# A decoder layer with a product-key expert layer: U and V rows of three token blocks gathered as pairs into 18 slots, their weighted sums on TensorE

## What is computed

```
q = (xt @ w_query).reshape(T, 8, 2, 128)
s = einsum('thcd,hckd->thck', q, sub_keys)
top_s, top_i = top_k(s, 16)                    # per head and half of the query: the 16 best of 128 keys
cand_s = top_s[:, :, 0, :, None] + top_s[:, :, 1, None, :]
best_s, pos = top_k(cand_s, 16)                # 16 of 256 pairs: 16 experts out of 16384, per head
gate = softmax(best_s)
u = expert_u[expert_idx]; h = gelu(einsum('cd,ced->ce', xc, u))
out = einsum('ce,ced->cd', gate * h, expert_v[expert_idx])
x = layer_norm(alpha * x + out)
```

## Time and profile before

| | |
|---|---|
| median of three runs | 1891.44 us |
| span of the profiled execution | 1889.7 us |
| PE, DVE, POOL, ACT busy | 67%, 68%, 57%, 13% |
| DMA engines, packets of the gathers | 77.2% of 16 engines' span |
| all DMA | 603.28 MB, mean 319 GB/s |
| granted PE clock, mean | 0.82 |

### The profile page before, as it was taken

How to read it: one execution, slowest core, us unless ns; L and a number is a source line. 1 busy time by engine, 2 the same in 40 slices (tenths; PEclk the granted TensorE clock), 3 DMA queues, 4 the chain that set the end, 5 groups by cost and what they waited for, 6 DMA issues and landing times.

```text
span 1889.7 us, 14555 instructions
## 1 busy us (share of the span) xinstructions
PE 1258.4 (67%) x3056; PEld 582.3 (31%) x3056; DVE 1289.4 (68%) x2842; ACT 238.6 (13%) x570; POOL 1073.2 (57%) x1253
## 2 busy tenths in 40 slices
PE   6778979563789776456666565665656565566665
PEld 3565446231346432122222221222222222222221
DVE  1348988789668866666767676767576667666556
ACT  0110000112111111011100111100101011111110
POOL 0004344335446667657767666667676767667774
PEclk9889989676989888777777878777877887778787
DMA  7668787857589889889999998899999999899996
GB/s 267 239 245 321 300 316 278 295 181 277 212 284 386 296 311 365 313 313 355 360 348 356 345 363 308 322 352 349 361 349 344 348 369 335 323 345 358 350 369 262
DMA packets 180946, 603.28 MB, mean 319 GB/s; under 512 B 18720, under 2 KB 21024, under 8 KB 180768
## 3 DMA queue, kind: packets, MB, share of 16 engines
q0 software_dynamic: 147456, 536.94, 77.2%
q1 hardware_dynamic: 33440, 65.80, 9.6%
HBM read 600.57 MB, written 2.10 MB: 319 GB/s over the span
## 4 chain that ended last, share of the span: by engine, by line
PE 24%; issue 20%; DVE 18%; DMA 17%; POOL 15%; another core or an unknown queue 1%; ACT 1%; POOLq 1%; DVEq 0%; SPq 0%; ACTq 0%
POOL ring L376 14%; DMA ring<-peer_v,stage 10%; PE ACC L428 9%; DVE ring L953 6%; PE W L483 6%; DMA ring<-peer_u,stage 6%; PE W L489 2%; PE W L659 2%; PE X L631 2%; DMA wt<-w_in 1%; PE ACC L631 1%; PE W L631 1%; DVE best_i L1207 1%; DVE xs L1001 1%
## 5 line engine op out<-in xcount | busy, mean ns | idle before, releaser
L428 PE MATMUL ACC<-ring,diag 128*128 128x512 f32 x1272 | 783.5, 774 | 476.6 <-DMA ring<-peer_v,stage 442.1
L953 DVE SCALAR_TENSOR_TENSOR ring<-ring,X 128x1024 f32<-128x1024 f32 x512 | 613.3, 1219 | 316.0 <-DMA ring<-peer_u,stage 288.1
L376 POOL DMA_INDIRECT ring<-peer_u,stage x512 | 522.1, 1020 | 410.1 <-DVE ring L953 214.1
L376 POOL DMA_INDIRECT ring<-peer_v,stage x512 | 503.0, 982 | 246.0 <-issue 153.8
L428 PEld LDWEIGHTS ACC<-ring,diag 128*128 128x128 f32 x1272 | 298.5, 248 | 956.7 <-issue 889.8
L771 ACT ACTIVATE diag<-ident,gate 128x128 f32<-128x128 f32 x318 | 122.8, 399 | 895.3 <-PE ACC L428 627.2
L1001 DVE SCALAR_TENSOR_TENSOR xs<-ring,gate,xs 128x1024 f32<-128x1024 f32 x96 | 123.3, 1284 | 53.6 <-DMA ring<-peer_v,stage 45.0
L483 PE MATMUL W<-wt,actT 128*128 128x512 f32 x320 | 143.9, 607 | 12.6 <-DMA ident<-ident_in 11.5
L659 PE MATMUL W<-actT,wt 128*128 128x128 f32 (+1 forms) x512 | 116.4, 389 | 1.4 <-ACT actT L833 1.4
L973 DVE SCALAR_TENSOR_TENSOR xs<-ring,gate,xs 128x512 f32<-128x512 f32 x98 | 73.3, 748 | 47.8 <-DMA ring<-peer_v,stage 45.7
L659 PEld LDWEIGHTS W<-actT,wt 128*128 128x128 f32 x512 | 80.1, 198 | 36.7 <-issue 2.7
(11 more groups left out here) (180 smaller groups left out, 804.3 us busy)
## 6 DMA issues: line engine op xcount, KB each, us to landing
wt<-w_in SPq DMA_DIRECT2D x14, 2048.0 KB
wt<-peer_w_query SPq DMA_DIRECT2D x8, 2048.0 KB
wt<-w_out SPq DMA_DIRECT2D x4, 2048.0 KB
ring<-peer_u,stage POOLq DMA_INDIRECT x512
ring<-peer_v,stage POOLq DMA_INDIRECT x512
out<-xs SPq DMA_DIRECT2D x4, 512.0 KB, 5.4
actT<-xT SPq DMA_DIRECT2D x1, 1536.0 KB, 11.7
xs<-x SPq DMA_DIRECT2D x1, 1536.0 KB, 14.1
```

What stands on the lines that cost most here:

```text
L376: pool.indirect_dma_start(out=ring[:, r, :], out_offset=None, in_=table, in_offset=bass.IndirectOffsetOnAxis(ap=stage[:, half, c:c + 1], a ...
L428: last = nc.tensor.matmul(ACC[:, half * HW:(half + 1) * HW], diag[:, odd, m, :], ring[:, r, half * HW:(half + 1) * HW], start=start and m ...
L953: STT(out=ring[:, r, :], in0=ring[:, r, :], scalar=1.0, in1=X[:], op0=ALU.mult, op1=ALU.mult, accum_out=hid[:, bass.ds(e, 1)]).then_inc(sl ...
```

## The change

**Tables.** U and V are laid side by side in one table `uv` of 16384 x 2048 floats before the launch. The kernel sees it as 32768 rows of 4 KB, with U of expert e in row 2e and V in row 2e + 1; the index is doubled by one more small DVE instruction per quarter, and a V gather has `element_offset` 1024.

**Buffers.** One `arena` of 18 slots of 8 KB per partition. The mixer's buffers and the ring of 8 are views of it. Once the mixer and block 0 are done with them, the slots are used for blocks 1 to 3.

**Block 0** keeps the ring, now for all its 16 groups of V rows; the last five have three rows on PE and five on DVE.

**Blocks 1 to 3** are 384 pairs. For each, POOL issues a U gather into the first half of a slot and a V gather into the second, both with the index read straight from `idx`, with one wait per pair (`pairs_summed` of the pair 18 before). DVE takes the dot. After four pairs (`FG`) ACT takes the GELU of four columns, DVE multiplies them by the gates (`weigh`, placed behind the first dot of the next group), ACT makes four diagonals in a ring of six (`ND`), and PE adds all four V rows. DVE adds no V row of these blocks. The steps that find experts lie between groups of four.

```diff
+V_GROUPS = E // RING
+AT_V = U_GROUPS
+ALONE = 11
+
+
+
+NF = (NB - 1) * E
+NS = 18
+EARLY, LATE = 6, 14
+FG = 4
+ND = 6
...
         wt = sb("wt", [P, NW, KD, HW])
...
-        ring = sb("ring", [P, RING, D])
-        attn = sb("attn", [P, 3 * HW])
+        arena = sb("arena", [P, NS * 2 * D])
+        fused = [arena[:, i * 2 * D:(i + 1) * 2 * D] for i in range(NS)]
...
+        keys = part(7 * K, K, "p (c n) -> p c n", c=HC)
+        wt = part(8 * K, 4 * K, "p (i k n) -> p i k n", i=NW, k=KD)
+        actT = part(12 * K, 2 * K, "p (k t) -> p k t", k=KD)
+        ring = part(14 * K, 4 * K, "p (r d) -> p r d", r=RING)
...
         ACC = ctx.enter_context(nc.psum_tensor("ACC", [P, D], fp32))
+        X2 = W[:, 0:2, :].rearrange("p a n -> p (a n)")
+        ACC2 = W[:, 2:4, :].rearrange("p a n -> p (a n)")
+
+        def token_of(b):
+
+            return X2 if b == 2 else X[:]
+
+        def sum_of(b):
+
+            return ACC2 if b % 2 else ACC[:]
...
+                    pool.indirect_dma_start(
-                    one_table(peer_u, quarter * QUARTER + j * RING, n, j % 2, n)
+                    one_table(0, quarter * QUARTER + j * RING, n, j % 2)
             for i in range(V_GROUPS):
                 n = AT_V + i
-                one_table(peer_v, i * RING, n, n % 2, n)
-            with pool.Fori(0, MIXED // PERIOD) as quarter:
-                pool.wait_ge(experts_ready, quarter + 5)
-                for j in range(PERIOD):
-                    both_tables(quarter * QUARTER + (E + j * HALF), quarter * QUARTER + (E - LAG + j * HALF),
-                                quarter * PERIOD + (AT_MIXED + j), (AT_MIXED + j) % 2,
-                                quarter * (2 * PERIOD) + (AT_MIXED + 2 * j))
-            for i in range(TAIL):
-                n = AT_TAIL + i
-                one_table(peer_v, NB * E - LAG + i * RING, n, n % 2, AT_MIXED + 2 * MIXED + i)
+                one_table(D, i * RING, n, n % 2)
+            for n in range(NF):
+                slot = n % NS
+                if n % QUARTER == 0:
+                    pool.wait_ge(experts_ready, 4 + n // QUARTER + 1)
+                if n == 0:
+                    pool.wait_ge(mixer_ready, 2 * NB)
+                elif n == EARLY:
+                    pool.wait_ge(keys_scored, 4 + 3 * WQ)
+                elif LATE <= n < NS:
+                    for r in (2 * (n - LATE), 2 * (n - LATE) + 1):
+                        pool.wait_ge(slot_used[r], AT_V + V_GROUPS + 1)
+                elif n >= NS:
+                    pool.wait_ge(pairs_summed, n - NS + 1)
+                pool.indirect_dma_start(
+                    out=fused[slot][:, 0:D], out_offset=None, in_=rows,
+                    in_offset=bass.IndirectOffsetOnAxis(ap=idx[:, E + n:E + n + 1], axis=0),
+                ).then_inc(pair_landed[slot], 16)
+                pool.indirect_dma_start(
+                    out=fused[slot][:, D:2 * D], out_offset=None, in_=rows,
+                    in_offset=bass.IndirectOffsetOnAxis(ap=idx[:, E + n:E + n + 1], axis=0),
+                    element_offset=D,
+                ).then_inc(second_landed[slot], 16)
...
+            def add_pairs(b):
+
+                if b > 1:
+                    pe.wait_ge(sum_read, b - 1)
+                for n in range((b - 1) * E, b * E):
+                    first, last_one = n % E == 0, n % E == E - 1
+                    pe.wait_ge(pair_diag_ready, n + 1)
+                    pe.wait_ge(second_landed[n % NS], 16 * (n // NS + 1))
+                    for half in range(2):
+                        last = nc.tensor.matmul(
+                            sum_of(b)[:, half * HW:(half + 1) * HW], fdiag[:, n % ND, :],
+                            fused[n % NS][:, D + half * HW:D + (half + 1) * HW], start=first, stop=last_one)
+                    last.then_inc(pairs_summed, 1)
...
+            beside(range(2 * ALONE + sum(BESIDE_QUERY), 2 * V_GROUPS))
+            for b in range(1, NB):
+                add_pairs(b)
 
...
-                if b:
-
-                    last_dot(b * 4 - 1)
                 if b == 1:
                     act.wait_ge(x1_taken, 2 * NB)
+                elif b == 2:
+                    act.wait_ge(scores_stored, 4 + 3 * WQ)
+                elif b == 3:
+                    act.wait_ge(pair_dotted, E)
                 for half in range(2):
-                    last = nc.scalar.activation(X[:, half * HW:(half + 1) * HW], xs[:, b, half * HW:(half + 1) * HW],
...
+            def gate_exp(q):
+
+                cols = slice(q * QUARTER, (q + 1) * QUARTER)
+                act.wait_ge(experts_ready, q + 1)
+                nc.scalar.activation(gate[:, cols], gate[:, cols], ACT.Exp).then_inc(pair_gate_ready, 1)
+
+            def pair_group(g):
+
+                cols = slice(E + g * FG, E + (g + 1) * FG)
+                act.wait_ge(pair_dotted, (g + 1) * FG)
+                nc.scalar.activation(hid[:, cols], hid[:, cols], ACT.Gelu).then_inc(pair_gelu_ready, 1)
+                act.wait_ge(pair_weighed, g + 1)
+                for n in range(g * FG, (g + 1) * FG):
+                    if n == 0:
+                        act.wait_ge(slot_used[PE_SLOTS[-1]], AT_V + V_GROUPS + 1)
+                    elif n >= ND:
+                        act.wait_ge(pairs_summed, n - ND + 1)
+                    nc.scalar.activation(fdiag[:, n % ND, :], ident[:], ACT.Copy,
+                                         scale=gate[:, E + n:E + n + 1]).then_inc(pair_diag_ready, 1)
 
             project(0, WAVES[0])
...
-                mixed_diagonals(first, first + 1)
-                gelu(q - 1, q)
-                mixed_diagonals(first + 1, first + 2)
-                act.wait_ge(weights_ready, q - 3)
-                mixed_diagonals(first + 2, first + PERIOD)
-            gelu(4 * NB - 1, 4 * NB)
-            for i in range(TAIL):
-                if i == 1:
-                    act.wait_ge(weights_ready, 4 * NB - 3)
-                diagonals(AT_TAIL + i, (AT_TAIL + i) % 2, lambda r: NB * E - LAG + i * RING + r)
+            beside(range(2 * ALONE + sum(BESIDE_QUERY), 2 * V_GROUPS))
+            gate_exp(4)
+            gate_exp(5)
+            for g in range(NF // FG):
+                pair_group(g)
+                if g % 8 == 6 and g // 8 + 6 < 4 * NB:
+                    gate_exp(g // 8 + 6)
+                if g % 32 == 16 and g // 32 + 2 < NB:
+                    token_to_psum(g // 32 + 2)
 
         @block.vector
...
+            def pair_dot(n):
+
+                b = 1 + n // E
+                slot = n % NS
+                dve.wait_ge(pair_landed[slot], 16 * (n // NS + 1))
+                STT(out=fused[slot][:, 0:D], in0=fused[slot][:, 0:D], scalar=1.0, in1=token_of(b), op0=ALU.mult,
+                    op1=ALU.mult, accum_out=hid[:, E + n:E + n + 1]).then_inc(pair_dotted, 1)
+
+            def weigh(g):
+
+                cols = slice(E + g * FG, E + (g + 1) * FG)
+                dve.wait_ge(pair_gelu_ready, g + 1)
+                TT(out=gate[:, cols], in0=gate[:, cols], in1=hid[:, cols], op=ALU.mult).then_inc(pair_weighed, 1)
+
+            def gate_norm(q):
+
+                dve.wait_ge(pair_gate_ready, q - 3)
+                g = gate[:, q * QUARTER:(q + 1) * QUARTER].rearrange("p (h k) -> p h k", h=2)
+                link(nc.vector.reduce_sum(gsum[:, 0:2], g, AX.X))
+                link(nc.vector.reciprocal(gsum[:, 0:2], gsum[:, 0:2]))
+                link(TT(out=g, in0=g, in1=gsum[:, 0:2].unsqueeze(2).to_broadcast([P, 2, TOPK]), op=ALU.mult))
...
+                if b == 0:
+                    for r in (DVE_SLOTS[-1], PE_SLOTS[-1]):
+                        dve.wait_ge(slot_used[r], AT_V + V_GROUPS + 1)
+                    TT(out=xs[:, b, :], in0=xs[:, b, :], in1=sum_of(b), op=ALU.add).then_inc(sum_read, 1)
                 else:
-                    n, slots = AT_TAIL + TAIL, (DVE_SLOTS[-1], PE_SLOTS[-1])
-                for r in slots:
-                    dve.wait_ge(slot_used[r], n + 1)
-                TT(out=xs[:, b, :], in0=xs[:, b, :], in1=ACC[:], op=ALU.add).then_inc(sum_read, 1)
+                    dve.wait_ge(pairs_summed, b * E)
+                    STT(out=xs[:, b, :], in0=xs[:, b, :], scalar=ALPHA, in1=sum_of(b), op0=ALU.mult,
+                        op1=ALU.add).then_inc(sum_read, 1)
                 dve.wait_ge(sum_read, b + 1)
...
-                STT(out=idx[:, at:at + n], in0=sel[:, 0, :], scalar=float(P), in1=sel[:, 1, :],
+                link(TS(sel[:, 1, :], sel[:, 1, :], 2.0, None, ALU.mult))
+                STT(out=idx[:, at:at + n], in0=sel[:, 0, :], scalar=2.0 * P, in1=sel[:, 1, :],
                     op0=ALU.mult, op1=ALU.add).then_inc(experts_ready, 1)
...
-            tail(1, TAIL)
+            retrieve(1, 1)
+            gate_norm(4)
+            gate_norm(5)
+            for g in range(NF // FG):
+                for n in range(g * FG, (g + 1) * FG):
+                    if n % E == 0:
+                        dve.wait_ge(token_in_psum, n // E + 2)
```

(17 more changed lines are left out.)

212 lines of the change are left out of this document (59 added, 153 removed).

## The result

The changed kernel takes 1832.35 us (1829.79 to 1834.73), the kernel before beside it on the same chip 1890.28 us: a ratio of 0.969, 95% interval [0.967, 0.971]. The forecast was 1731 us with a range of 1700 to 1825, so the time lies 7 us above the range. The direction was right; of the 160 us that were promised, 58 came. The profiled execution is the run of 1829.79 us and has a span of 1827.7 us.

A forecast was written before the change was run, and what follows sets the result against it. Gathers set the pace, held back by too few outstanding; afterwards POOL's issuing would bind. 703.5 us unchanged + 999 for 768 gathers + 4.9 landing + 21.5 end = 1729, plus 1.7 for the median: 1731 us, range 1700 to 1825.

The forecast's parts named there:

- Up to 703.5 us: nothing.: Mixer and block 0: time unchanged, with POOL free for the pairs at 703.5 us.
- POOL's cost of a gather: Blocks 1 to 3: 1.001 us per gather on POOL plus a 0.30 us gap, 1.301 us.
- The DMA engines' cost.: Blocks 1 to 3: between 1.276 and 1.413 us per gather; the lower taken, so POOL's 1.301 us decides, 999 us.
- theory G: From the experiments, not the prediction: each gather takes 1.40 us on a path shared with engines' increments, whatever its rows' size.
- The stretches of the earlier trace: Mixed stage before the change: 11 and 20 us at 411 and 403 GB/s, taken as showing what the DMA engines can do.
- How long a slot is held: about 20 us of 47, so the stalls go.: Blocks 1 to 3: slots held about 20 us, POOL up to 47 us ahead, so expert searches no longer delay gathers.
- DVE and PE: Blocks 1 to 3: DVE under 62 us per quarter against 83 of gathers; PE at most 10.0 us per group of four.
- The end: After the last gather's issue: 4.9 us to land, then 21.5 us for last dot, sums, join, norm and store.
- The first: Rival for blocks 1 to 3: DMA stays at 371 GB/s on scattered rows, 1.413 us per gather, 1817 us; chance 0.19.
- PE's clock: Rival for the sums on PE: clock stays at 1.2 GHz, 3.5 us per row, 2091 us, slower; chance 0.04.
- the hand-back of slots as such: Rival for blocks 1 to 3: slots held 47 us, gathers 1.525 us apart, no change at 1903 us; chance 0.04.
- the table side by side: Rival for the gathers: interleaved U and V rows read worse, bounded at 1.52 us per gather, about 1900 us; chance 0.03.

The follow-up runs named there:

- the chain kernels: Kernels without the layer: small copies on VectorE (in one also ScalarE), each waiting for the increment before, beside gathers or loads; the last took 459.58 us.
- the kernel with 8 KB gathers: The changed kernel with one gather of 8 KB rows per pair instead of two of 4 KB: 1700.55 us, ratio 0.898.
- the half rows: The changed kernel with V gathers of blocks 1 to 3 fetching 2 KB of a row in place of 4 KB: 1842.89 us, ratio 0.972.

## Why the prediction was right and wrong

- **"Up to 703.5 us: nothing."** Right: the first gather of a pair starts at 703.86 us, the first dot at 727.01 (forecast: near 727), the first sums run from 733.37 for 9.58 us (forecast: end near 739, it was 743).
- **"POOL's cost of a gather", 1.301 us.** Too high: 0.946 + 0.30 = 1.25 us. In the sum that would have been 42 us to the good, and none of it arrived.
- **"The DMA engines' cost. I take the lower one, 1.276 us."** For the DMA engines this was right: 409 to 411 GB/s with gathers back to back, in the kernel (408 over 16 us) and in the chain kernels, and 276 GB/s at a share of 0.82 with smaller rows. **The step that failed is the conclusion, "Then POOL's 1.301 us decides: 768 x 1.301 = 999 us."** A third limit stood above both: with gathers closer than 1.40 us, increments come late and the slots with them. The term was 768 x 1.426 = 1095 us, 96 us more. By theory G 768 x (1.40 - 1.301) = 76 us of these are the limit itself; the other 20 us would be holes after stops that are not made up, which no run singles out.
- **What the trace before could have told.** Its gathers averaged 1.52 us, but two groups of eight without a stop start 10.89 us apart, 1.36 us per gather, already under 1.40. The sign is there as well, twice and faintly, in the timeline of DVE; here is the longer one: as in the changed kernel, four MAX8 are followed by an instruction that needs only them and starts 3.04 us late.

```profile
1362.65 0.85 DVE L1206 MAX8 best_v<-cand 128x8 f32<-128x128 f32 x4
1366.54 0.09 DVE L1207 MATCH_VALUE_LOAD best_i<-best_v,cand 128x8 f32 x1 [3.04 <-remote]
```

- **The stretches of the earlier trace rows.** They were read rightly as "the engines can do 411", and wrongly as "the kernel can run there". POOL issued only 8 gathers in the 11 us. In the 20 us it issued 6; the rest were gathers still queued and 2 MB of loads, of 8 MB in all. The chain kernel shows that the first 15 gathers of a run at full pace cost nothing. They were too short to show what comes behind.
- **"How long a slot is held: about 20 us of 47, so the stalls go."** With prompt increments that is borne out (the kernel with 8 KB gathers never leaves the DMA engines idle). With late ones the first search of the stage is already caught: DVE waits 7.38 us for its own results at 744.46, POOL stands 13.09 us before 773.06, and the window 770 to 780 us has 149 GB/s, where I wanted none near 200.
- **DVE and PE.** 62 of 83 us and 10.0 us per group were fair: neither engine was at its limit in the stage. PE came to 70% and DVE to 60% of the stage, for want of rows; in the 8 KB kernel 79 and 69%, against the forecast's 80 and 70. A group of four behind a rest took 7.13 to 10.19 us.
- **"The end": 26.4 us** from the last gather's start. It was 1827.7 - 1797.7 = 30.0, with a 7.27 us remote wait of ACT in it.
- **The rivals.** The first (371 GB/s, 1817 us, chance 0.19) is nearest in number, 15 us short, and wrong in cause: bytes at 371 GB/s would have made the half rows faster and the 8 KB rows no faster. That the range reached almost to the measured time was owed to this rival, not to the mechanism. (The upper end of the forecast, 1.35 us, lies 0.44 of the way from 1.301 to the rival's 1.413, not a third.) PE's clock (0.83 of full speed in the stage), the hand-back of slots as such and the table side by side cost nothing that shows: the same table feeds the 421 GB/s.
- **The rule of the Trainium skill that spoke against the change** (358 GB/s from HBM) did not hold for this one core, with 421 GB/s over 890 us. Another of its rules would have pointed the right way: "DMA: Bandwidth & Descriptors", section "Measured (HBM→SBUF, 128 partitions, SWDGE, issued from GpSimd)", advises batches of 1 MiB or more. The pair as one gather is 1 MiB and won; the page's reason, small transfers being inefficient, is not the one here, since gathers of 512 KB back to back reached 410 GB/s.

The change gained what it could on the way from 1.52 us per gather to the limit: 768 x (1.519 - 1.426) = 71 us, less 10 for a longer end (from 18.7 to 29.1 us after the last gather's issue), against the 62 us between the two spans.
